# Seven products for the early chunks too, with weights ordered ahead of page reads

## Chip, cores, metric

The kernel runs on one core of a Trainium2 chip. The metric is the device time of one execution in microseconds (us). The program is written by hand for each engine: TensorE (PE in the profile), VectorE (DVE), ScalarE (ACT), GpSimd (POOL) and SyncE (SP, which here only issues transfers). Engines wait for each other through semaphores.

## What is computed

Two layers (DEPTH = 2) of a hybrid decoder trunk run over 512 prompt tokens and 8 x 8 sample tokens, 576 columns in all, in float32. Cut to what matters:

```python
h = rmsnorm(x, norm_g)
proj = h @ w_in                       # 1024 -> all branches at once
(lru_x, lru_z, nsa_q, nsa_kv, nsa_z, nsa_g,
 dn_qkv, dn_z, dn_a, dn_b, merge_g) = split(proj)
u = causal_conv(lru_x)                # 4 taps
out_lru = (rg_lru(u) * silu(lru_z)) @ w_lru_out
out_nsa = (sparse_attention(nsa_q, nsa_kv, pages, window) * silu(nsa_z)) @ w_nsa_out
qkv = silu(causal_conv(dn_qkv))       # 1536 channels, 4 taps
out_dn = (rmsnorm(gated_delta(l2norm(q), l2norm(k), v)) * silu(dn_z)) @ w_dn_out
merged = sum(sigmoid(merge_g_i) * out_i)
x = x + merged @ w_out
```

The sample rows also attend to a paged cache (8 pages of 128 rows for each of 8 samples) and to a window of 512 rows. Keys, values, states and convolution tails are outputs too.

## The kernel before

**The dense stream.** The projection is cut into chunks of 128 output channels. The list `UNITS` gives the order of all dense work of a layer: small gates and lx, then lz (4 chunks), dc (12), q (4), kv (6), nz (4), dz (4), then the merge gates mg with the output products ow between them, then wo. A unit fills one PSUM bank with 128 x 288 results, and units alternate between two banks (`u % 2`), so unit u waits until unit u - 2 is evicted by the engine named in the list ("A" for ACT, "V" for DVE). `dense()` yields after each matmul step (two records in the trace), and PE's program pulls steps from it with `fill(n, end)` and `dense_to(end)` between the small matmuls of the other stages. `take_to(end)` in ACT's and DVE's program evicts all units up to `end`; an engine takes them exactly where its program says so.

**Two ways to a pair of chunks.** For lx, lz and dc each chunk has two units (halves of the columns) of 8 steps: 32 steps to two chunks. For the kinds in `PAIRED` (q, kv, nz, dz, mg) two chunks are one 2 x 2 block product in seven products instead of eight (`PRODUCTS = "1627543"`), each of 4 steps: 28 steps. That needs sums of the activations (T2, T3, T4 in `tt`, and B12 - B11, written over B12), made once per layer, and sums of weights made by DVE for each pair: `weight_sums` (L1865) makes three in `ws` and in the ring slot, and runs right after product "5" of the pair before; `weight_sum` (L1874) makes the fourth after product "6". The results come out by additions of products in `sg` (L1783, L1786). DVE takes five of the seven products, ACT two.

**Weights.** `ring` holds two slots of two chunks each (1 MB), `owr` two output weights. SP's `weights(n)` (L593) waits until the pair in slot n - 2 is done (`slot_done`), `out_weights(n)` (L612) likewise for n - 2. SP works through its program in order, and the same program reads the cache: `cached_keys` (L650) and `cached_values` (L655) issue 16 transfers each with an address read from the page table, `window_keys` (L658) and `window_values` (L661) one per sample.

**Stages of a layer.** First the early stage: lx, lz and dc chunks with the convolutions (`conv`, L1847; `mix`, L1997, one per dc chunk) and the LRU recurrence on DVE, gates and SiLU on ACT. Then q, kv, nz, dz under the delta rule, then the rotary multiplies, then prompt attention (slots, L1292 to L1339), then the sample stage: four rounds of k2 with two samples each (L1371 to L1460). A round reads keys first, values later, and pulls 44 dense steps: the output products of one pair and the seven products of the next mg pair. `dext` is a ring of 7 chunk buffers that `mix` reads.

Of the kernel before, what the change touches and what calls it, by code (L numbers as in the profile page):

```python
# [138 lines left out]
EXTN = 7  # L139
# [64 lines left out]
def products(kind, c):  # L204
# [10 lines left out]
         + [(kind, c, h, who) for kind, n, who in (("lz", 4, "A"), ("dc", 12, "A")) for c in range(n) for h in range(2)]  # L215
         + [unit_ for kind, n in (("q", 4), ("kv", 6), ("nz", 4), ("dz", 4)) for c in range(0, n, 2) for unit_ in products(kind, c)]
# [20 lines left out]
PAIRED = ("q", "kv", "nz", "dz", "mg")  # L237
PAIRS = [(kind, c) for kind, c in SLOTS if kind in PAIRED]
NSUM = 4 + 4 * len(PAIRS)
# [30 lines left out]
def summed(l, k, which):  # L270

    return l * NSUM + {"first": 6, "S2": 7 + 4 * k, "S4": 8 + 4 * k}[which]

# [17 lines left out]
def chained(eng, done):  # L291
# [34 lines left out]
    s_pw=4, s_tr=8, s_tb=4, s_ta=4, s_mix=4, s_or=4, s_ot=4, s_z=8, dh_t=1, conv_ok=12, silu_ok=5, dc_ok=1, sp_abs=2,  # L326
    sp_exp=3, gb_ok=1, bm_ok=10, s0_in=128, p_z=5, p_y=5, p_g=20, p_e=5, p_x=5, p_s=5, p_d=5, p_k=15, p_b=5, i_w=31,
    i_wm=31, i_x=31, i_xm=31, f_mm=5, f_u=4, f_v=4, f_w=5, m_mm=3, u_mm=4, f_m=3, q_w=3, q_s=4, q_n=3, q_oe=4, b_gl=4,
    b_pe=7, b_so=1, b_vt=1, b_vn=1, b_vm=4, b_sn=4, dn_ok=1, mg_ok=32, small_in=96, sm_in=32, ln_ok=5, sum_ok=88,
# [3 lines left out]
def hybrid_trunk(nc, dram, out):  # L333

    ctx = ExitStack()
    with ctx:
# [178 lines left out]
        T2, T3, T4 = (tt[:, k] for k in range(3))  # L515
        S2, S3 = ws[:, 0], ws[:, 1]
# [5 lines left out]
        def factors(n, which):  # L522
# [32 lines left out]
        def chunk_half(kind, c, h):  # L555

            if kind == "kv":
                return hh(qk7[:, 4 + c // 2] if c % 2 == 0 else vT[:, c // 2], h)
            return hh(qk7[:, c] if kind == "q" else zs[:, {"nz": 4, "dz": 8}[kind] + c], h)
# [5 lines left out]
        def _(sp):  # L565
# [71 lines left out]
            for l in range(DEPTH):  # L637
# [43 lines left out]
                out_weights(l * NO + 3)  # L681
                sp.wait_ge(s["b_out"], l * 32 + 32)
# [162 lines left out]
        def _(pe):  # L845
# [11 lines left out]
            def dense():  # L857

                for u in range(DEPTH * N_ALL):
# [40 lines left out]
                    elif kind in PAIRED:  # L900
# [3 lines left out]
                        elif h == "6":  # L904
                            pe.wait_ge(s["sum_ok"], summed(l, k, "S2" if k else "first"))
                        elif h == "5" and k == 0:
                            pe.wait_ge(s["sum_ok"], summed(l, 0, "S2"))
                        elif h == "3":
                            pe.wait_ge(s["sum_ok"], summed(l, k, "S4"))
                        w, x = factors(g, h)  # L910
# [80 lines left out]
            for l in range(DEPTH):  # L991
# [24 lines left out]
                dense_to(u0 + U_DC + 4)  # L1016
# [3 lines left out]
                for n in range(8):  # L1020
# [9 lines left out]
                    fill(2, u0 + U_Q)  # L1030
# [447 lines left out]
        def _(act):  # L1478
# [32 lines left out]
            for l in range(DEPTH):  # L1511
# [3 lines left out]
                def take_to(end):  # L1515

                    for u in range(gone[0], end):
# [10 lines left out]
                        if kind == "lz":  # L1528
                            ins = A(hh(zs[:, c], h), ps, ACT.Silu)
                        elif kind == "dc":  # L1530
                            if h == 0 and c == 0 and u >= N_ALL:
                                act.wait_ge(s["xs_out"], 16 * (u // N_ALL))
                            if h == 0 and c >= EXTN:
                                act.wait_ge(s["conv_ok"], past["conv_ok"] + c - EXTN + 1)
                            e = dext[:, c % EXTN]
                            if h == 0:
# [861 lines left out]
```

## Time and profile before

| | |
|---|---|
| median of 3 runs | 2092.81 us (2089.54 to 2092.93) |
| the profiled execution | 2090.35 us, span on the core 2088.5 us |
| granted TensorE clock, mean | 0.945 |
| PE / DVE / ACT busy | 1842.8 / 946.0 / 515.9 us |
| HBM read / written | 153.67 / 21.71 MB |

In the profile a busy PE is one whose matmuls are in flight; "SPq" rows are transfers that SP issues, with the time the issuing takes. Bracketed figures in a timeline are the idle time before the row and what ended it.

### The profile page before, as it was taken

How to read it: one execution, taken by the hardware profiler on the slowest of the kernel's cores; microseconds unless marked ns; L12 is line 12 of the kernel's file. 1: busy time of each engine (PE TensorE's matmuls, PEld its weight loads, DVE VectorE, ACT ScalarE, POOL GpSimd, SP SyncE). 2: the span in 40 equal slices, each digit the busy share in tenths (PEclk: the TensorE clock that was granted, in tenths of full speed). 3: DMA queues.
4: the chain of work that ended last, by engine and by line, in shares of the span. 5: the costliest groups of instructions: out<-in, count | busy, mean ns of one | idle time of the engine just before them, and what ended most of it. 6: DMA issues, size and time to landing. Idle time of an engine off the chain costs nothing.

```text
span 2088.5 us, 29550 instructions
## 1 busy us (share of the span) xinstructions
PE 1842.8 (88%) x11486; PEld 1323.4 (63%) x11486; DVE 946.0 (45%) x2208; ACT 515.9 (25%) x1161; POOL 91.5 (4%) x133
## 2 busy tenths in 40 slices
PE   7999999998499955599999999999984998655999
PEld 5777787875355644477467767888652556444763
DVE  2558546336265432243135675453462653333421
ACT  3143211123266310110112341111322662110100
POOL 0001000011000000000000010100120000000000
PEclk9999999989799987899999999999997999887999
DMA  6214111123410233426042141111333103443321
GB/s 214 67 60 106 42 42 42 56 72 85 129 51 11 82 110 101 133 89 187 1 162 64 61 106 42 26 37 56 109 92 104 31 11 93 123 118 97 113 88 46
DMA packets 196528, 170.07 MB, mean 81 GB/s; under 512 B 49248, under 2 KB 186898, under 8 KB 195942
## 3 DMA queue, kind: packets, MB, share of 16 engines
q1 hardware_dynamic: 192164, 150.11, 24.7%
q0 software_dynamic: 4064, 18.03, 2.7%
q8 instruction: 91, 1.49, 0.3%
q14 instruction: 47, 0.39, 0.1%
q10 hardware_dynamic: 162, 0.05, 0.0%
HBM read 153.67 MB, written 21.71 MB: 84 GB/s over the span
## 4 chain that ended last, share of the span: by engine, by line
PE 75%; DVE 10%; SPq 7%; issue 4%; DMA 3%; ACT 1%; ACTq 0%; DVEq 0%
PE PS L920 49%; PE PS L849 5%; SPq L643 3%; DVE arena L1854 3%; DMA ring<-in_w_in 3%; SPq L655 3%; PE PS L1292 2%; PE PS L1305 2%; PE PS L1140 1%; PE PS L1122 1%; DVE arena L1780 1%; PE PS L1142 1%; PE PS L1361 1%; PE PS L1211 1%; PE PS L1026 1%
## 5 line engine op out<-in xcount | busy, mean ns | idle before, releaser
L920 PE MATMUL PS<-hT,ring 128*128 128x288 f32 x2624 | 692.3, 411 | 6.4 <-DVE arena L2057 3.7
L920 PEld LDWEIGHTS PS<-hT,ring 128*128 128x128 f32 x2624 | 488.4, 191 | 143.9 <-issue 11.7
L920 PE MATMUL PS<-zs,owr 128*128 128x288 f32 x768 | 215.6, 424 | 126.2 <-DVE sg L1786 126.2
L920 PEld LDWEIGHTS PS<-zs,owr 128*128 128x128 f32 x768 | 143.5, 197 | 170.5 <-DVE sg L1786 127.6
L920 PE MATMUL PS<-tt,ws 128*128 128x288 f32 x672 | 190.4, 415 | 11.8 <-DVE sg L1910 4.4
L849 PE MATMUL PS<-con,arena 128*128 128x128 f32 (+5 forms) x934 | 148.5, 286 | 13.4 <-DMA arena<-in_nsa_k_norm 10.7
L849 PEld LDWEIGHTS PS<-con,arena 128*128 128x128 f32 (+5 forms) x934 | 111.6, 144 | 74.2 <-issue 46.0
L920 PEld LDWEIGHTS PS<-tt,ws 128*128 128x128 f32 x672 | 120.7, 190 | 51.9 <-DVE sg L1910 8.0
L1786 DVE TENSOR_TENSOR ws<-ring 128x512 f32<-128x512 f32 x84 | 58.1, 691 | 201.8 <-DMA ring<-in_w_in 200.3
L920 PE MATMUL PS<-arena 128*128 128x512 f32 (+1 forms) x320 | 124.8, 594 | 2.1 <-DVE sg L1910 2.1
L1783 DVE TENSOR_TENSOR sg<-PS,sg 128x288 f32<-128x288 f32 x132 | 60.3, 457 | 134.6 <-PE PS L920 132.6
L920 PE MATMUL PS<-tt,ring 128*128 128x288 f32 x336 | 103.6, 443 | 11.3 <-DVE sg L1783 11.3
L1292 PE MATMUL PS<-arena 64*128 64x128 f32 (+3 forms) x256 | 53.1, 493 | 60.0 <-ACT arena L1713 60.0
L1854 DVE SCALAR_TENSOR_TENSOR arena<-arena,par 128x512 f32<-128x512 f32 x192 | 99.5, 518 | 6.8
L1713 ACT ACTIVATE arena<-PS,sm 128x128 f32<-128x128 f32 (+3 forms) x128 | 66.8, 524 | 128.6 <-DVE sm L2251 122.6
L920 PEld LDWEIGHTS PS<-arena 128*128 128x128 f32 (+1 forms) x320 | 52.9, 180 | 70.9 <-issue 67.9
L920 PEld LDWEIGHTS PS<-tt,ring 128*128 128x128 f32 x336 | 65.4, 205 | 32.4 <-DVE sg L1783 12.2
L2251 DVE CUSTOM_DVE_ANT_0 PS<-PS,con 128x128 f32<-128x128 f32 (+3 forms) x128 | 61.9, 505 | 44.2 <-PE PS L1292 44.2
L1292 PEld LDWEIGHTS PS<-arena 64*128 64x128 f32 x256 | 20.1, 193 | 85.9 <-ACT arena L1713 67.8
L1704 ACT ACTIVATE arena<-arena,sm 128x128 f32<-128x128 f32 (+3 forms) x128 | 64.7, 553 | 23.2 <-DVE sm L1780 23.2
L1786 DVE TENSOR_TENSOR arena<-arena,PS 128x512 f32<-128x512 f32 (+3 forms) x70 | 43.4, 622 | 59.0 <-PE PS L1142 36.7
L1780 DVE TENSOR_TENSOR arena<-arena 128x2304 f32<-128x2304 f32 (+3 forms) x24 | 39.7, 1656 | 58.1 <-ACT arena L1594 22.2
(303 smaller groups left out, 2060.9 us busy)
## 6 DMA issues: line engine op xcount, KB each, us to landing
ring<-in_w_in SPq DMA_DIRECT2D x54, 1024.0 KB, 5.4
arena<-in_cache_nsa_kv SPq DMA_DIRECT2D x128, 192.0 KB, 2.5
ring<-in_w_in SPq DMA_DIRECT2D x32, 256.0 KB, 4.3
arena<-in_state_nsa_win SPq DMA_DIRECT2D x32, 256.0 KB, 3.3
arena<-in_cache_nsa_kv SPq DMA_DIRECT2D x128, 64.0 KB, 1.8
arena<-in_w_out SPq DMA_DIRECT2D x4, 2048.0 KB, 8.1
out_win_sample<-in_state_nsa_win POOLq DMA_DIRECT2D x2, 4032.0 KB, 23.1
arena<-in_x_prompt SPq DMA_DIRECT2D x8, 512.0 KB, 5.3
```

Of the source, the lines that this page charges most:

```text
L643: at_page = sp.value_load(pgt[0:1, b * PAGES + k:b * PAGES + k + 1], min_val=0, max_val=N_PHYS - 1)
L655: sp.dma_start(page(b % 2, k)[:, 3 * P:4 * P], page_of(b, k)[:, 3 * P:4 * P]).then_inc(s["cv_in"], 16)
L849: return nc.tensor.transpose(dst, src, ident[0:src.shape[0], 0:src.shape[0]])
L920: ins = mm(to, w, x, start=start, stop=stop, skip_group_check=True)
L1292: mm(PS[:, 4 + g, 0:q0 + P], qk7[m, r, q0:q0 + P], qk7[m, 5 + br, 0:q0 + P], start=True, stop=True).then_inc(s["a_s"], 1)
L1704: A(p, p, ACT.Copy, scale=sm8[:, 7, u % 8:u % 8 + 1]).then_inc(s["a_n"], 1)
L1713: A(pring[slot % PRING][:, 0:width], PS[:, 4 + slot % 2, 0:width], ACT.Exp, scale=-1.0, bias=sm8[:, 0, k:k + 1], accum_out=sm8[:, 1, k:k + ...
L1780: return V.tensor_tensor(dst, a, b, ALU.mult)
L1783: return V.tensor_tensor(dst, a, b, ALU.add)
L1786: return V.tensor_tensor(dst, a, b, ALU.subtract)
L1854: ins = stt(out=d, in0=e, scalar=w(j), in1=d, op0=ALU.mult, op1=ALU.add)
L2251: V.tensor_tensor_reduce(out=raw, in0=raw, in1=C("causal")[:, 3 * P - q0:4 * P], scale=-1.0, scalar=-NEG, op0=ALU.add, op1=ALU.min, accum_ ...
```

## The change

The pairs of lz and dc join `PAIRED`, so that their 16 chunks are made by seven products each pair; "early" pairs (`k < N_EARLY`) take a separate T1 = B12 - B11, in `zs`, while lx units still read B12 whole; B12 itself is overwritten only at the first q pair. T1 to T4 are made before the lz chunks. DVE makes the early weight sums as it does for later pairs. ACT no longer evicts lz with SiLU but in a pass over `zs` later; products "5" and "3" of a dc pair are written to `dext` in two instructions. The steps of DVE's convolutions and LRU passes, and of ACT's activations, are cut into pieces with `take_to` between them. Mixes 10 and 11 move behind the first units of q. PE pulls three steps and not two after each LRU gate matmul. In the rotary multiplies DVE takes units in between.

In SP's program the weights move ahead: `weights(22)` before the wait for rotated keys, output weights and `weights(23)` between the first cached keys and values, and in each round of k2 `weights(25 + k2)` ahead of the wait for the keys, and the output weights between keys and values.

```diff
-         + [(kind, c, h, who) for kind, n, who in (("lz", 4, "A"), ("dc", 12, "A")) for c in range(n) for h in range(2)]
-         + [unit_ for kind, n in (("q", 4), ("kv", 6), ("nz", 4), ("dz", 4)) for c in range(0, n, 2) for unit_ in products(kind, c)]
+         + [unit_ for kind, n in (("lz", 4), ("dc", 12), ("q", 4), ("kv", 6), ("nz", 4), ("dz", 4)) for c in range(0, n, 2) for unit_ in products(kind, c)]
...
-PAIRED = ("q", "kv", "nz", "dz", "mg")
+PAIRED = ("lz", "dc", "q", "kv", "nz", "dz", "mg")
...
+        T1 = zs[:, 4:6, :].rearrange("p c (h t) -> p (c h) t", h=2)
...
-                    "4": (quarter(n, 1, 1), T4), "5": (quarter(n, 1, 0), B12), "6": (S2, T2), "7": (S3, T3)}[which]
+                    "4": (quarter(n, 1, 1), T4), "5": (quarter(n, 1, 0), T1 if early else B12), "6": (S2, T2), "7": (S3, T3)}[which]
...
+                weights(l * NS + 22)
                 sp.wait_ge(s["b_out"], l * 32 + 32)
                 sp.wait_ge(s["dn_ok"], past["dn_ok"] + 1)
                 sp.wait_ge(s["qk_ok"], past["qk_ok"] + 2)
                 cached_keys(0)
                 window_keys(0)
+                out_weights(l * NO + 4)
+                out_weights(l * NO + 5)
+                weights(l * NS + 23)
                 cached_values(0)
                 window_values(0)
-                for g in (22, 23, 24):
-                    weights(l * NS + g)
-                    for o in range(2):
-                        out_weights(l * NO + 2 * (g - 20) + o)
+                out_weights(l * NO + 6)
+                out_weights(l * NO + 7)
+                weights(l * NS + 24)
+                out_weights(l * NO + 8)
+                out_weights(l * NO + 9)
...
                 for k2 in range(DEC_BATCH // 2):
+                    weights(l * NS + 25 + k2)
                     if k2 < DEC_BATCH // 2 - 1:
                         sp.wait_ge(s["s_t"], past["s_t"] + 6 * (k2 + 1))
                         cached_keys(k2 + 1)
                         for b in (2 * k2 + 2, 2 * k2 + 3):
                             window_keys(b)
+                    for o in range(2):
+                        out_weights(l * NO + 10 + 2 * k2 + o)
+                    if k2 < DEC_BATCH // 2 - 1:
                         sp.wait_ge(s["s_pv"], past["s_pv"] + k2 + 1)
                         cached_values(k2 + 1)
                         for b in (2 * k2 + 2, 2 * k2 + 3):
                             window_values(b)
-                    weights(l * NS + 25 + k2)
-                    for o in range(2):
-                        out_weights(l * NO + 10 + 2 * k2 + o)
...
-                    fill(2, u0 + U_Q)
+                    fill(3, u0 + U_Q)
...
+                            elif kind == "dc" and h == "4":
+                                ins = sub(dext[:, (c + 1) % EXTN, HIST:HIST + HALF], sg[:, 2], ps)
+                            elif kind == "dc":
+                                e, summand = (dext[:, (c + 1) % EXTN], sg[:, 2]) if h == "5" else (dext[:, c % EXTN], sg[:, 1])
+                                cut = SEQ - HALF
+                                add(e[:, HIST + HALF:HIST + SEQ], ps[:, 0:cut], summand[:, 0:cut])
...
+                weight_sums(l, 0)
...
-                mix(0)
-                mix(1)
+                take_to(u0 + U_DC + 7)
+                mix(0, (8, 8, 9, 9))
+                mix(1, (10, 10, 11, 11))
+                take_before("lgp", 8)
                 dve.wait_ge(s["lg"], past["lg"] + 8)
-                link(mul(lb[:], lb[:], lu[:]))
+                for c in range(4):
+                    mul(lb[:, c], lb[:, c], lu[:, c])
+                    if c % 2:
+                        take_to(u0 + U_DC + 13 + c // 2)
+                mix(2, (15, 15, 16, 16))
+                mix(3, (17, 17, 18, 18))
...
+                mix(4, (22, 22, 23, 23))
+                mix(5, (24, 24, 25, 25))
...
-                link(V.tensor_tensor_scan(lh.rearrange("p c t -> p (c t)"), la.rearrange("p c t -> p (c t)"),
-                                          lb.rearrange("p c t -> p (c t)"), 0.0, ALU.mult, ALU.add))
...
+                for c in range(4):
+                    link(V.tensor_tensor_scan(lh[:, c], la[:, c], lb[:, c], 0.0, ALU.mult, ALU.add))
+                    ins = mul(zs[:, c], zs[:, c], lh[:, c])
+                    if c < 3:
+                        take_to(u0 + U_DC + 29 + c)
...
-                for c in range(3, 12):
-                    if c == 11:
-                        weight_sums(l, 0)
-                    mix(c)
+                mix(6, (32, 32, 33, 33))
+                mix(7, (34, 34, 35, 35))
+                mix(8, (36, 36, 37, 37))
+                mix(9, (38, 39, 40, 41))
+                take_to(u0 + U_Q)
                 dve.wait_ge(s["pj"], u0 + U_Q)
+                dve.wait_ge(s["sum_ok"], summed(l, N_EARLY, "S2"))
                 sub(B12, B12, B11).then_inc(s["sum_ok"], 1)
+                mix(10, (43, 43, 44, 44))
+                mix(11, (45, 45, 46, 46))
...
                 mul(zs[:, 8:12], zs[:, 8:12], dc[:, 0:4]).then_inc(s["dn_ok"], 1)
+                normed = began[("bc_ok", past["bc_ok"] + 10)]
+                take_to(normed + 1)
...
                     if n == 0:
                         take_before("kt_t", 2)
+                    else:
+                        take_to(normed + 2)
                     link(mul(x, x, rep(C("cos"), m - n)))
```

## Rows read from the trace of the kernel before

**Rows 1.** Waits of the whole trace: us in total, times, longest us.
```profile
DVE ws L1786 <- DMA ring<-in_w_in: 200.3, 10, 27.2
...
PE PS L920 <- DVE sg L1786: 126.2, 6, 21.8
```

**Rows 2.** Timeline of PE, sample stage of layer 0: start, length, instruction.
```profile
698.43 1.96 PE L1371 MATMUL PS<-arena,con 128*32 128x128 f32 x64 [0.84 <-issue]
...
735.18 1.95 PE L1371 MATMUL PS<-arena,con 128*32 128x128 f32 x64
...
758.49 2.29 PE L920 MATMUL PS<-zs,owr 128*128 128x288 f32 x4 [20.77 <-DVE sg L1786]
...
795.24 1.96 PE L1371 MATMUL PS<-arena,con 128*32 128x128 f32 x64
```

**Rows 3.** Timeline of DVE, attention and sample stages of layer 0.
```profile
561.95 0.69 DVE L1786 TENSOR_TENSOR ws<-ring 128x512 f32<-128x512 f32 x1 [26.98 <-DMA ring<-in_w_in]
...
731.29 0.46 DVE L1783 TENSOR_TENSOR sg<-PS,sg 128x288 f32<-128x288 f32 x1 [1.01 <-PE PS L920]
755.55 0.69 DVE L1786 TENSOR_TENSOR ws<-ring 128x512 f32<-128x512 f32 x1 [23.80 <-DMA ring<-in_w_in]
```

**Rows 4.** Timeline of SP's issues, the same stages.
```profile
520.05 17.25 SPq L650 DMA_DIRECT2D arena<-in_cache_nsa_kv  x16
...
556.24 0.51 SPq L610 DMA_DIRECT2D ring<-in_w_in  x1
...
707.70 17.15 SPq L650 DMA_DIRECT2D arena<-in_cache_nsa_kv  x16
724.89 0.99 SPq L658 DMA_DIRECT2D arena<-in_state_nsa_win  x2
729.86 17.22 SPq L655 DMA_DIRECT2D arena<-in_cache_nsa_kv  x16
...
748.16 0.51 SPq L610 DMA_DIRECT2D ring<-in_w_in  x1
748.71 1.58 SPq L626 DMA_DIRECT2D owr<-in_w_dn_out  x2
```

**Rows 5.** Timeline of PE, rotary multiplies and attention of layer 0.
```profile
503.43 4.04 PE L920 MATMUL PS<-tt,ring 128*128 128x288 f32 x8 [5.64 <-DVE sg L1783]
507.31 2.10 PE L920 MATMUL PS<-hT,ring 128*128 128x288 f32 x8
...
566.02 0.80 PE L1292 MATMUL PS<-arena 64*128 64x128 f32 x4 [28.96 <-ACT arena L1713]
```

**Rows 6.** Windows after two stops: length, busy PE, PEld, DVE, ACT, POOL, clock, DMA.
```profile
566.00:574.00 8.00, 7.98 (x32) 5.08 (x33) 3.35 (x17) 3.94 (x15) 0.00 (x0) 0.62 0.00 0
...
758.00:764.00 6.00, 5.51 (x17) 4.06 (x18) 2.08 (x4) 0.93 (x2) 0.00 (x0) 0.57 0.00 0
```

**Rows 7.** Window over most of the early stage of layer 0.
```profile
88.00:188.00 100.00, 100.00 (x414) 78.48 (x413) 67.00 (x151) 34.71 (x62) 0.00 (x0) 1.00 0.23 63
```

**Rows 8.** Timeline of PE, early stage of layer 0.
```profile
44.38 58.47 PE L920 MATMUL PS<-hT,ring 128*128 128x288 f32 x240
...
188.05 0.27 PE L849 MATMUL PS<-con,cst 128*27 128x128 f32 x1
```

**Rows 9.** Timeline of DVE, early stage of layer 0.
```profile
141.33 2.55 DVE L1780 TENSOR_TENSOR arena<-arena 128x2304 f32<-128x2304 f32 x1
...
144.60 4.96 DVE L2037 TENSOR_TENSOR_SCAN arena<-arena 128x2304 f32<-128x2304 f32 x1
...
156.62 0.17 DVE L1999 COPY arena<-arena 128x24 f32<-128x24 f32 x1
...
161.00 0.17 DVE L1999 COPY arena<-arena 128x24 f32<-128x24 f32 x1
...
187.27 0.69 DVE L1786 TENSOR_TENSOR ws<-ring 128x512 f32<-128x512 f32 x1
...
189.21 0.17 DVE L1999 COPY arena<-arena 128x24 f32<-128x24 f32 x1
```

More of the change, by code:

```diff
@@ L270, in summed, with product_unit @@
 def summed(l, k, which):
-    return l * NSUM + {"first": 6, "S2": 7 + 4 * k, "S4": 8 + 4 * k}[which]
+    return l * NSUM + (8 + 4 * N_EARLY if which == "T1" else
+                       {"S2": 7, "S4": 8}[which] + 4 * k + (k > N_EARLY or k == N_EARLY and which == "S4"))
+def product_unit(l, k, which):
+    return l * N_ALL + FIRST[PAIRS[k]] + PRODUCTS.index(which)
 def merged(n):
@@ L1015, in _ @@
                 ins.then_inc(s["gt_t"], 1)
-                dense_to(u0 + U_DC + 4)
+                dense_to(u0 + U_DC + AHEAD)
                 pe.wait_ge(s["con_in"], CON_IN * l + 16)
@@ L1527, in take_to @@
                         ps = PS[:, u % 2, 0:HALF]
[L1528 to L1536, printed above, removed]
-                                ins = A(e[:, HIST:HIST + HALF], ps, ACT.Copy)
-                            else:
-                                A(e[:, HIST + HALF:HIST + SEQ], ps[:, 0:SEQ - HALF], ACT.Copy)
-                                ins = A(e[:, HIST + SEQ:EXT].rearrange("p (b t) -> p b t", t=S_EXT)[:, :, HIST:],
-                                        ps[:, SEQ - HALF:HALF].rearrange("p (b t) -> p b t", t=DEC_SEQ), ACT.Copy)
-                        elif h == "1":
+                        if h == "1":
                             act.wait_ge(s["pv"], taken(u - 1, "V"))
@@ L1547, in take_to @@
                             ins = A(sg[:, 0], ps, ACT.Tanh, scale=0.5)
+                        elif kind == "dc":
+                            if c == 0 and u >= N_ALL:
+                                act.wait_ge(s["xs_out"], 16 * (u // N_ALL))
+                            if c >= EXTN:
+                                act.wait_ge(s["conv_ok"], past["conv_ok"] + c - EXTN + 1)
+                            ins = A(dext[:, c % EXTN, HIST:HIST + HALF], ps, ACT.Copy)
                         else:
@@ L1862, in conv @@
                                 link(ins)
+                        take_to(units[j])
                 def weight_sums(l_, k):
@@ L1983, in _ @@
                 V.memset(dext[:, :, 0:HIST], 0.0)
+                dve.wait_ge(s["sum_ok"], past["sum_ok"] + 2)
+                sub(T4, T2, B21).then_inc(s["sum_ok"], 1)
+                sub(T1, B12, B11).then_inc(s["sum_ok"], 1)
                 take_to(u0 + U_LZ)
                 dve.wait_ge(s["pv"], taken(u0 + U_LZ, "V"))
+                weight_sums(l, 0)
                 for c in range(4):
-                    conv(lu[:, c], lext[:, c], lambda j: prm("lconv", 4 * j + c), prm("lcb", c), s["u_ok"])
+                    conv(lu[:, c], lext[:, c], lambda j: prm("lconv", 4 * j + c), prm("lcb", c), s["u_ok"],
+                         [u0 + U_LZ + min(4 * c + j, U_DC - U_LZ) for j in range(CONV_W)])
                 def tails(dst, ext):
@@ L1995, in _, with mix @@
                     tails(cst[:, c], lext[:, c])
-                def mix(c):
+                def mix(c, units):
                     e = dext[:, c % EXTN]
@@ L2005, in mix @@
                         ins.then_inc(s["dc_ok"], 1)
-                    conv(dc[:, c], e, lambda j: prm("dconv", 12 * j + c), None, s["conv_ok"])
+                    conv(dc[:, c], e, lambda j: prm("dconv", 12 * j + c), None, s["conv_ok"], [u0 + U_DC + at for at in units])
                 x = spb[:, 5, :].rearrange("p (k h) -> p k h", h=DN_H)
@@ L2012, in _ @@
                 stt(out=spb[:, 0, :], in0=spb[:, 5, :], scalar=-1.0, in1=spb[:, 5, :], op0=ALU.mult, op1=ALU.max).then_inc(s["sp_abs"], 1)
-                for n, (dst, a, b, op) in enumerate(((T3, B22, B12, sub), (T2, T3, B11, add), (T4, T2, B21, sub))):
-                    if n:
-                        dve.wait_ge(s["sum_ok"], past["sum_ok"] + n)
-                    op(dst, a, b).then_inc(s["sum_ok"], 1)
+                take_to(u0 + U_DC + 2)
                 dve.wait_ge(s["sp_exp"], past["sp_exp"] + 3)
@@ L2192, in _ @@
                         take_before("kt_t", 3)
+                    else:
+                        take_to(normed + 3)
                     add(x, x, y).then_inc(s["qk_ok"], 1)
```

95 lines of the change are left out of this document (62 added, 33 removed).

## Prediction

> **What bounds the kernel now.** The waits come first. TensorE (PE) is the busiest engine, and six times it stands still before the products `PS<-zs,owr`, 126.2 us in all, behind a weight sum of VectorE (DVE); DVE itself stands ten times, 200.3 us in all, for `ring<-in_w_in` to land [rows 1]. No other wait of PE is of that size, so I read the timeline at those places.
>
> The sample stage runs in four rounds of k2. Its first matmuls (L1371) start at 698.43, 735.18 and 795.24: the first round takes 36.75 us, the second 60.06, for the same work [rows 2]. In the second PE stops for 20.77 us before 758.49 [rows 2]. DVE took a product at 731.29, and then waited 23.80 us for the ring, until 755.55 [rows 3]: `take_to` runs `weight_sums` of the next pair right after product 5, and in order. SyncE (SP) shows why the ring is late: it issues 16 cached keys at 707.70 (17.15 us), window keys at 724.89, 16 cached values at 729.86 (17.22 us), and only at 748.16 the weights, at 748.71 the two output weights [rows 4]. The slot of those weights had been free since the round began; they stand behind 32 page reads. So PE waits for DVE, DVE for a transfer, and the transfer for its place in SP's program.
>
> The same happens once in the attention stage: weights are issued at 556.24 behind keys that began at 520.05 [rows 4], DVE waits 26.98 us for them [rows 3], PE 28.96 us [rows 5]. A smaller stop of another kind, 5.64 us before 503.43, ends with a product taken by DVE [rows 5], which was in the rotary multiplies.
>
> Each stop costs more than its length. After the two long ones the granted clock was 0.62 in 566 to 574 and 0.57 in 758 to 764, with PE busy nearly throughout [rows 6]: PE started at 1.2 GHz and came back to 2.4 some 5 to 7 us later.
>
> The early stage, where the new products go, is different. PE is busy 100.00 of 100 us there at full clock, DVE 67.00 [rows 7]. It goes from 56.1 (44.38 and three units of 3.9 us) to 188.05 [rows 8], 131.9 us.
>
> **The change, part by part, for one layer.** Layer 1 repeats layer 0, so everything counts twice.
>
> *Fewer matmuls.* 240 records take 58.47 us, 0.2436 each, two records to a matmul step [rows 8]. A pair of chunks now takes 4 units of 8 steps, and will take 7 units of 4: 28 instead of 32. Eight pairs (lz 2, dc 6) drop 32 steps, 32 x 0.487 = 15.6 us. PE alone would need 131.9 - 15.6 = 116.3 us, 13.6 to a pair.
>
> *More for DVE in those same microseconds.* A pair costs five evictions at 0.46 [rows 3], a fourth sum at 0.69, and three sums of which 187.27 to 189.21 shows the length, 1.94 [rows 9]: 4.9 us, and about 0.3 for two evictions that are split in two in dc. ScalarE (ACT) loses its evictions, which it had time for anyway. A `mix` takes 161.00 - 156.62 = 4.38 us [rows 9]; a pass over four LRU chunks 2.55, the scan 4.96 [rows 9]. From the third dc pair on, DVE owes, between the units that it must take:
> - pair 3: mixes 2 and 3 (8.8), the pair (5.2), two LRU passes (5.1): 19.1
> - pair 4: mixes 4 and 5 (8.8), 5.2, one pass (2.6): 16.5
> - pair 5: mixes 6 and 7 (8.8), 5.2, small steps (0.9), scan (5.0), one pass (2.6): 22.4
> - pair 6: mixes 8 and 9 (8.8), 5.2: 14.0
>
> That is 72.0 us against 4 x 13.6 = 54.6 of PE. There are two PSUM banks, so PE can lead by two units at most, and it waits for the other 17.4 us. In the four pairs before, DVE's load (two convolutions or two mixes and the products, 13 to 15 us a pair) lies inside PE's time, stretched in the second dc pair by the LRU gates; only the very first weight sums hold PE up, about 0.7. So the early stage takes 116.3 + 17.4 + 0.7 = 134.4 us, 2.5 more than before: the saved matmuls are spent on waiting for DVE. Mixes 10 and 11 then fall behind the stage, together with the moved B12 difference, so that `conv_ok` 12, the last SiLU and the squares come some 5 us later relative to the q pair; PE has other units to fill there, and I take 1.5. Sum: +4. Bounds: -12 if DVE's steps overlap so well that PE sets the pace after all (then only the first sums and the q pair cost), +12 if each of the 24 handovers of these pairs costs DVE some 0.3 us more than rows of undisturbed runs show.
>
> *Weights ahead of page reads.* In a round without a stop PE needs 36.75 us. SP's load per round is 17.2 + 1.0 + 17.2 + 1.0 + 0.5 + 1.6 = 38.5 us [rows 4]. I walk it from S, the start of the first round. `weights(25)` goes before S, since its slot is free. Keys S+9.3 to S+26.5 (as 707.70 is to 698.43), window keys to 27.5, output weights to 29.1, values from S+31.4 (729.86) to 48.6, window values 49.6, then `weights(26)` 50.1, keys to 67.3, window keys 68.3, output weights 69.9, values to 87.1, and once more the same to 106.8 for the last keys and 108.4 for output weights. PE starts rounds at S+36.75, 73.5 and 110.25. It wants keys at the start, which were issued by 27.5, 68.3 and 106.8; ring weights (through DVE) 33 us into a round, issued 20 us before that; values some 26 us into a round, with more than 10 us to spare; output weights about 2 us into a round, issued by 29.1, 69.9, 108.4 and hence 3 to 4 us ahead of need in the last round, about what a landing takes. So the three stops go, and SP, slower than PE by 1.8 us a round, just keeps ahead for the three rounds. Saved: second round 60.06 - 36.75 = 23.3, which holds the stop and the 2.5 of low clock behind it, three times: 70; I give back 1 for the last output weights: 69. Bounds 56 (5 us left in each round) and 71.
>
> *Weights 22 before the wait for keys.* Slot 20 is free after the matmuls at 507.31 (2.10 us), ahead of the keys at 520.05 [rows 4, 5], so the weights land before DVE asks. The stop of 28.96 goes, and the 3.4 lost at a clock of 0.5 after it: 32.4. What is late next is the output weights of that pair, now behind 16 keys and not 32 transfers: issued at 538 to 539, wanted at about 542. I take 31, bounds 26 and 32.4.
>
> *Takes between the rotary multiplies.* The product that ended the 5.64 us stop is taken right after the gating product; a later one waits about 2 us behind a multiply, and rotated rows come some 3 us later. I take 4 of the 5.64 plus low clock, bounds 0 and 7.
>
> Per layer: +4 - 69 - 31 - 4 = -100; two layers -200. The profiled execution took 2090.35 (span 2088.5), which gives 1890; the median of the runs shown is 2.5 above it, so 1892.
>
> **A rule that speaks against it.** The early stage would have many short stops of PE where it has none now. The rows show full clock where PE never stops [rows 7] and the lower one behind stops of 20 us and more [rows 6]; stops of 1 to 3 us, as forecast here, have no row of their own. The Trainium skill (TensorE: Matmul & The Clock Gate, section "A second HAM failure mode: psum-queue depth-cycling") says that cycling through PSUM banks with small idles between groups of matmuls can make the clock oscillate between its two levels. By that rule this stage would fall to the lower clock again and again, which is the third rival below; I take full clock, since each unit between two stops is 1.95 us of dense matmuls.
>
> **Rivals.**
> 1. The early stage keeps its 15.6 us (DVE overlaps after all): -12 instead of +4 per layer, 1892 - 32 = 1860. For it: DVE has 33 idle us in 100 there [rows 7]. Against: the added work is uneven, and three of the last four pairs hold more than a pair's time.
> 2. SP becomes the bound in the sample stage. It has 38.5 us of issues for 36.75 of PE; the weights share queues with page reads. If each of the six later rounds keeps 5 us, and the attention stop another 4, the time is 1892 + 30 + 8 = 1930.
> 3. The lower clock holds in dc pairs 3 to 6. A pair then takes PE 27.3 us instead of DVE's 18.0, so 9.3 x 4 x 2 = 74: 1966, if it holds throughout; 1930 at half of that.
> 4. Slower than before. SP's order puts `out_weights` between keys and values, and `weights(23)`, which waits for slot 21, ahead of the first values. Should such a wait close a ring (values late, so PE late, so the slot late), each round would be paced by it. It decides only beyond the 23.3 us that a round saves: values would have to land 34 us later than in the walk. Paced at 65 us a round it gives 1892 + 6 x 28 = 2060, and with the attention stop kept 2120. Nothing in the walk comes near it.
> 5. The reordering does nothing, because the transfer and not its issue is late: 1892 + 200 = 2092 or so. Against: 7 us pass from issue to DVE's start (748.16 to 755.55) [rows 3, 4], and 17 in SP's issues.
>
> **How the numbers follow.** Chances: the forecast 0.55, rival 1 0.15, rival 2 0.18, rival 3 0.08, rivals 4 and 5 0.04 together. The reordering's gain is common to the first four cases. The forecast's own bounds, not all at once, reach from 1870 to 1920; the range takes in rival 1 and most of rival 2 and leaves the lower clock out: 1858 to 1932. Faster by over 0.2% (about what a measurement of this kernel can tell from no change) 0.96, within it 0.015, slower 0.025.
>
> **What would show it.** L1371 starts about 37 us apart in all rounds, DVE's waits for `ring<-in_w_in` nearly gone from 200 us, granted clock 1.00 from 510 us on through the stage; these carry 180 of the 200 us. In the early stage PE busy near 85%, with waits for DVE (sums, stt lines of the convolution) from the third dc pair on, and the q pair starting 2 to 3 us later than 188 us. If PE is busy throughout there, rival 1 holds. If the granted clock falls below 1.00 there, rival 3. If PE stops before `owr` products for a DMA and not for DVE, rival 2. The prediction is wrong if the sample rounds differ from each other by more than 5 us.

## The result and the profile after

| | before | after |
|---|---|---|
| median | 2092.87 us (4 runs) | 1903.22 us (1899.25 to 1905.93, 4 runs) |
| profiled execution, span | 2090.35, 2088.5 us | 1899.25, 1897.5 us |
| granted clock, mean | 0.945 | 0.989 |
| PE / DVE busy | 1842.8 / 946.0 us | 1805.1 / 1021.6 us |

The ratio is 0.9093, 95% interval 0.9073 to 0.9114: 190 us less. The forecast was 1892, range 1858 to 1932.

The waits of the whole trace come first, as in [rows 1]: us in total, times, longest us. The first three rows are PE's largest, then come the one of the rotary multiplies and the row of DVE that had 200.3 us.

```profile
PE PS L933 <- DVE arena L1802: 11.7, 6, 2.5
PE PS L933 <- DVE arena L2115: 11.0, 2, 5.5
PE PS L933 <- DVE sg L1799: 10.8, 11, 2.3
...
PE PS L933 <- DVE sg L1802: 4.2, 2, 2.1
...
DVE ws L1802 <- DMA ring<-in_w_in: 1.8, 2, 1.2
```

The weights have gone from 200.3 us of DVE's waiting to 1.8, and PE's 126.2 us behind weight sums are gone with them. New are waits of another kind, for evictions (L1799, L1802) and for a copy at L2115. Now PE's timeline, layer 0, at the places of [rows 2], [rows 5] and [rows 8].

```profile
43.83 13.85 PE L933 MATMUL PS<-hT,ring 128*128 128x288 f32 x56
...
130.06 2.21 PE L933 MATMUL PS<-tt,ring 128*128 128x288 f32 x8 [0.57 <-DVE sg L1799]
132.10 2.10 PE L933 MATMUL PS<-hT,ring 128*128 128x288 f32 x8
136.68 3.90 PE L933 MATMUL PS<-hT,ring 128*128 128x288 f32 x8 [2.48 <-DVE arena L1802]
140.41 2.10 PE L933 MATMUL PS<-tt,ws 128*128 128x288 f32 x8
...
168.05 2.21 PE L933 MATMUL PS<-tt,ring 128*128 128x288 f32 x8 [2.28 <-DVE sg L1799]
...
175.15 2.21 PE L933 MATMUL PS<-hT,ring 128*128 128x288 f32 x8 [2.24 <-DVE arena L1802]
...
190.76 0.27 PE L862 MATMUL PS<-con,cst 128*27 128x128 f32 x1
...
206.40 4.21 PE L933 MATMUL PS<-hT,ring 128*128 128x288 f32 x8 [5.49 <-DVE arena L2115]
...
509.78 1.24 PE L933 MATMUL PS<-zs,owr 128*128 128x288 f32 x4 [2.08 <-DVE sg L1802]
...
540.43 0.49 PE L1305 MATMUL PS<-arena 64*128 64x128 f32 x4 [1.89 <-ACT arena L1729]
...
670.16 1.96 PE L1384 MATMUL PS<-arena,con 128*32 128x128 f32 x64 [0.84 <-issue]
...
706.90 1.96 PE L1384 MATMUL PS<-arena,con 128*32 128x128 f32 x64
...
743.65 1.96 PE L1384 MATMUL PS<-arena,con 128*32 128x128 f32 x64
...
780.46 1.96 PE L1384 MATMUL PS<-arena,con 128*32 128x128 f32 x64
...
783.52 1.21 PE L933 MATMUL PS<-zs,owr 128*128 128x288 f32 x4 [0.52 <-DMA owr<-in_w_dn_out]
```

The rounds start 36.74, 36.75 and 36.81 us apart: the three long stops are gone, and so is that of 28.96 us in the attention, of which 1.89 us are left. The early stage, which had no stop, now has them, the longest 2.48 us.

SP's issues in the last round it feeds, to set against [rows 4]: keys, window keys, output weights, values, window values, ring weights.

```profile
760.90 17.05 SPq L657 DMA_DIRECT2D arena<-in_cache_nsa_kv  x16
778.00 0.98 SPq L665 DMA_DIRECT2D arena<-in_state_nsa_win  x2
779.02 1.05 SPq L633 DMA_DIRECT2D owr<-in_w_dn_out  x2
780.86 17.22 SPq L662 DMA_DIRECT2D arena<-in_cache_nsa_kv  x16
798.12 1.15 SPq L668 DMA_DIRECT2D arena<-in_state_nsa_win  x2
799.31 0.51 SPq L617 DMA_DIRECT2D ring<-in_w_in  x1
```

PE took these output weights at 783.52 after a wait of 0.52 us (above): SP is just in time, with nothing over.

Last the windows (columns as in [rows 6]): the quiet and the crowded part of the early stage, to set against [rows 7], then three short ones.

```profile
88.00:121.00 33.00, 33.00 (x137) 25.72 (x136) 23.08 (x65) 11.52 (x19) 0.00 (x0) 1.00 0.14 43
121.00:190.70 69.70, 57.59 (x219) 41.43 (x219) 66.77 (x153) 19.85 (x32) 0.00 (x0) 0.98 0.23 60
...
137.00:141.00 4.00, 4.00 (x11) 2.83 (x10) 3.85 (x11) 0.34 (x1) 0.00 (x0) 0.58 0.47 162
166.00:178.00 12.00, 6.83 (x25) 4.53 (x26) 11.44 (x33) 0.61 (x2) 0.00 (x0) 1.00 0.39 75
206.50:213.00 6.50, 6.50 (x27) 3.55 (x28) 2.33 (x4) 4.71 (x8) 6.38 (x12) 0.58 1.02 285
```

From 121 us on DVE is busy 66.77 of 69.70 us and PE 57.59: DVE sets the pace there. In these windows the clock is 1.00 but for one fall behind the stop of 2.48 us, and a second in the q pair. From 510 to 890 us, attention and sample stage, it was 1.00 throughout, as forecast.

**Where the time went, layer 0.** Each row is the difference of the same two landmarks in both traces.

| stretch | before | after | change | forecast |
|---|---|---|---|---|
| early stage, to the conv tails' matmul | 131.9 | 135.2 | +3.3 | +2.5 |
| q pair, to the first delta-rule matmul (223.0; 230.2) | 34.9 | 39.4 | +4.5 | +1.5 |
| to the output products behind the rotary multiplies (509.25; 509.78) | 286.3 | 279.6 | -6.7 | -4 |
| to the first round | 189.2 | 160.4 | -28.8 | -31 |
| rounds, to the first wo matmul (988.48; 890.89) | 290.1 | 220.7 | -69.3 | -69 |

The sum, with 0.6 us less ahead of the early stage, is -97.6 us; layer 1 gave -93.4 (its rounds -67.2). Of the -6.7 only 5.0 belong to the rotary multiplies (from 495.69 to 509.25 before, from 501.25 to 509.78 after). The other 1.6 lie in the delta rule, 272.7 us before and 271.1 after: both kernels have a stretch at half clock there (last section), and in layer 0 of the kernel before it was some 3 us longer.

### The profile page after: what moved, and what is told of

It reads as the page before. It is cut to its first block, busy times and chain, and to the rows that moved or that the text cites. A ratio compares the mean times of both kernels' runs of the same rounds, so it can differ in the third digit from the quotient of the medians.

```text
span 1897.5 us, 29614 instructions
## 1 busy us (share of the span) xinstructions
PE 1805.1 (95%) x11358; PEld 1283.6 (68%) x11358; DVE 1021.6 (54%) x2414; ACT 505.7 (27%) x1133; POOL 91.3 (5%) x133
## 4 chain that ended last, share of the span: by engine, by line
PE 77%; DVE 14%; SPq 4%; issue 3%; ACT 1%; DMA 0%; ACTq 0%; DVEq 0%
PE PS L933 50%; PE PS L862 5%; DVE arena L1871 3%; PE PS L1305 2%; PE PS L1318 2%; SPq L650 2%; DVE arena L1796 2%; PE PS L1153 1%; PE PS L1135 1%; DVE ws L1802 1%; PE PS L1155 1%; SPq L657 1%; PE PS L1224 1%; PE PS L1374 1%; PE PS L1246 1%
## 5 line engine op out<-in xcount | busy, mean ns | idle before, releaser
L933 PE MATMUL PS<-hT,ring 128*128 128x288 f32 x1984 | 549.3, 416 | 27.0 <-DVE arena L1802 11.7
L933 PEld LDWEIGHTS PS<-hT,ring 128*128 128x128 f32 x1984 | 366.8, 192 | 138.7 <-DVE arena L1802 14.4
L933 PE MATMUL PS<-tt,ws 128*128 128x288 f32 x928 | 259.1, 413 | 14.3 <-DVE sg L1928 4.4
L933 PEld LDWEIGHTS PS<-tt,ws 128*128 128x128 f32 x928 | 168.6, 190 | 70.5 <-issue 9.4
L1799 DVE TENSOR_TENSOR sg<-PS,sg 128x288 f32<-128x288 f32 x164 | 74.9, 457 | 147.7 <-PE PS L933 145.7
L933 PE MATMUL PS<-tt,ring 128*128 128x288 f32 x464 | 133.5, 423 | 7.5 <-DVE sg L1799 7.4
L1543 ACT ACTIVATE sg<-PS 128x288 f32<-128x288 f32 x58 | 23.4, 403 | 337.9 <-PE PS L933 337.7
L933 PEld LDWEIGHTS PS<-tt,ring 128*128 128x128 f32 x464 | 86.4, 195 | 36.2 <-DVE sg L1799 11.7
L933 PEld LDWEIGHTS PS<-arena 128*128 128x128 f32 (+1 forms) x320 | 52.7, 179 | 71.1 <-issue 68.1
L1802 DVE TENSOR_TENSOR ws<-ring 128x512 f32<-128x512 f32 x116 | 80.1, 691 | 3.9 <-DMA ring<-in_w_in 1.8
L1802 DVE TENSOR_TENSOR arena<-arena,PS 128x512 f32<-128x512 f32 (+3 forms) x70 | 43.3, 621 | 58.1 <-PE PS L1155 36.7
L1535 ACT ACTIVATE sg<-sg 128x288 f32<-128x288 f32 x72 | 31.2, 436 | 120.2 <-DVE sg L1799 105.1
```

The source lines that it names most:

```text
L933: ins = mm(to, w, x, start=start, stop=stop, skip_group_check=True)
L1799: return V.tensor_tensor(dst, a, b, ALU.add)
L1802: return V.tensor_tensor(dst, a, b, ALU.subtract)
```

## Experiments

**The order alone, and the rest alone.** Does the reordering carry the gain, and what do the products add?

```diff
 # order_only: the kernel before, with SP's program of the changed kernel
+                weights(l * NS + 22)
...
+                    weights(l * NS + 25 + k2)
...
 # products_only: the changed kernel, with SP's program of the kernel before
-                weights(l * NS + 22)
...
-                    weights(l * NS + 25 + k2)
...
```

> The kernel before with the new order of SyncE's transfers alone (weights 22 ahead of the keys, weights and output weights ahead of page reads in the rounds); no new products, no new takes. Theory (the order carries the whole gain): the sample stage of a layer loses 69 us and the attention stop 29 us, so 2093 - 2 x 98 = 1897 us, and DVE's waits for the ring go from 200 us to under 10. Rival (the order needs the other edits to pay, because the rotary takes or the products bring the keys forward): the stops go only in part, above 1930 us.

Measured: 1894.55 us, ratio 0.9055 (0.9032 to 0.9078). All long stops are gone, DVE waits 2.8 us in all for the ring, and the rotary stop is still there: PE's timeline of this kernel.

```profile
501.17 3.25 PE L926 MATMUL PS<-tt,ring 128*128 128x288 f32 x6 [5.64 <-DVE sg L1789]
```

> The changed kernel with the transfers in the old order. Theory (the early stage is bound by DVE, so the seven products cost about 8 us a layer up to the second q pair and the rotary takes give 6 to 7 back): 2090 to 2100 us, with the rounds of the sample stage 36.7, 60, 61 us again. Rival (the 15.6 us a layer of dropped matmuls are really saved and something later hides it): near 2062 us.

Measured: 2102.75 us, the median of six runs (2101.63 without one of 2141.53), ratio 1.005 (1.0027 to 1.0073), a little above what was expected. PE's timeline shows the early stop, the one of the q pair and one of the rounds.

```profile
137.06 1.24 PE L927 MATMUL PS<-hT,ring 128*128 128x288 f32 x4 [2.48 <-DVE arena L1796]
...
206.80 1.81 PE L927 MATMUL PS<-hT,ring 128*128 128x288 f32 x3 [5.50 <-DVE arena L2109]
...
761.64 2.29 PE L927 MATMUL PS<-zs,owr 128*128 128x288 f32 x4 [21.14 <-DVE sg L1796]
```

The two ratios multiply to 0.910, which is the changed kernel's: the parts hardly meet. The order brings the whole gain; all the rest together (products, rotary takes and the steps cut to make room for them) loses time.

**The takes in the rotary multiplies alone**, on top of the order.

```diff
 # order_only, and:
+                normed = began[("bc_ok", past["bc_ok"] + 10)]
+                take_to(normed + 1)
...
                         take_before("kt_t", 2)
+                    else:
+                        take_to(normed + 2)
...
```

> The kernel before with the new order of transfers and the takes between the rotary multiplies, lz and dc as before (32 steps for two chunks). Theory: the early stage returns to 131.9 us and the q pair to 22.3, so 1903 - 2 x 7.8 = 1888 us, faster than the changed kernel. Rival (the seven products pay after all): at or above 1903, up to 1903 + 31 = 1934 us.

Measured: 1885.62 us, ratio 0.9004 (0.8981 to 0.9028), 9 us below order_only on the same chip. The rotary stop is 2.08 us, as in the changed kernel. This version keeps eight plain units for a pair of early chunks, and is the fastest here together with lz_pairs (below): 12.2 us less in span than the changed kernel (1885.3 against 1897.5), 17.6 in the medians. The stretch of the q pair is 34.9 us again; the 22.3 of the expectation is not this stretch.

**The weight sums of the early pairs.** If DVE's sums are what costs the 15.6 us of saved matmuls, nearly free sums must bring them back. In this kernel each early sum is made over 4 of the 128 columns of a block, so the results of the early pairs are not those of the reference; PE, evictions and transfers are as in the changed kernel; `ws` is set to zero once, ahead of all.

```diff
+            V.memset(ws[:], 0.0)
...
+                    m = 4 if k < N_EARLY else P
...
-                    sub(S3, quarter(n, 0, 0), quarter(n, 1, 0)).then_inc(s["sum_ok"], 1)
+                    sub(S3[:, :, 0:m], quarter(n, 0, 0)[:, :, 0:m], quarter(n, 1, 0)[:, :, 0:m]).then_inc(s["sum_ok"], 1)
...
```

> The changed kernel, with the weight sums of the lz and dc pairs made of 4 columns in each of 4 blocks and not 128, so that the sums of the early pairs are left out in the main: 0.17 us and not 0.69 each, with the same waits and the same order. Theory (VectorE's load sets the early stage's pace): of the 17 us over PE's time some 2 us a pair go, the early stage falls from 135.2 to about 127 us, the total to about 1887 us. Rival (PE waits for the handovers between engines and for the places of the takes, not for the load): early stage within 2 us of 135, total 1900 to 1903 us.

Measured: 1885.39 us, ratio 0.9008 (0.8986 to 0.903). The early stage takes 56.9 to 183.53 us, 126.6. A window over its crowded part:

```profile
121.00:183.00 62.00, 54.45 (x215) 39.80 (x214) 59.11 (x150) 19.97 (x32) 0.00 (x0) 1.00 0.25 67
```

8.6 us come back, not 19 (135.2 down to the 116.3 of PE alone): DVE is busy 59.11 of 62.00 us even so. Evictions, mixes and LRU passes fill it. The stage is now 5.3 us shorter than with plain units (131.9), but in the q pair PE stops for 5.39 us here too, and that stretch takes 38.0 and 38.5 us in the two layers instead of 34.9. So in all, seven products with nearly free sums only tie with the plain units of order_rope.

**The order cut in two.** Its two places, each without the other, on the kernel before.

```diff
 # rounds_order: the loop over k2 only
+                    weights(l * NS + 25 + k2)
...
 # first_order: all that stands ahead of that loop only
+                weights(l * NS + 22)
...
```

> The kernel before with the new order in the four rounds of the sample stage only; the attention stage's transfers as before. Theory: the three long rounds of a layer fall to 36.8 us, 69 us a layer, 2094 - 138 = 1956 us, and the stop of 29 us in attention stays. Rival (the late weights of attention carry over, so that the rounds start behind): over 1970 us.

Measured: 1952.59 us, ratio 0.9336 (0.9311 to 0.9361).

> The kernel before with the new order up to the attention stage only (weights 22 ahead of the keys, output weights and weights 23 between keys and values); the rounds as before. Theory: the attention stop of 29 us and the low clock behind it go, two times 29 to 31: 2094 - 60 = 2034 us; rounds of 36.8, 60, 61, 60 us stay. Rival: the stop moves to the output weights or to a wait for the first values and the gain is under 10 us a layer, over 2074 us.

Measured: 2029.51 us, ratio 0.9709 (0.9688 to 0.973). The rounds of layer 0 stay as they were (36.8, 59.5 and 61.3 us). The two timelines, first rounds_order, then first_order, each with what its half leaves or mends:

```profile
562.99 0.80 PE L1293 MATMUL PS<-arena 64*128 64x128 f32 x4 [28.99 <-ACT arena L1714]
```

```profile
538.91 0.49 PE L1297 MATMUL PS<-arena 64*128 64x128 f32 x4 [1.89 <-ACT arena L1718]
```

The halves bring 138 and 61 us (from 2090.5), together the 199 of order_only; the forecast had 2 x 69 and 2 x 31.

**Only the ring's weights ahead in a round**, the output weights left behind the values.

```diff
 # order_only, but in the loop over k2:
-                    for o in range(2):
-                        out_weights(l * NO + 10 + 2 * k2 + o)
                     if k2 < DEC_BATCH // 2 - 1:
...
+                    for o in range(2):
+                        out_weights(l * NO + 10 + 2 * k2 + o)
```

> The kernel before with the new order, but in the rounds only the ring weights go ahead; the output weights are issued behind the cached values, as before. Theory of the walk: output weights are wanted 2 us into the next round and issued some 10 us after that, so PE stops about 16 us in each of three rounds for the transfer itself and not for DVE; of 69 us a layer about 21 are left, and 29 in attention: 1993 us. Rival (only the ring weights, through DVE's sums, hold the rounds up): 1895 us.

Measured: 1994.13 us, ratio 0.9533 (0.9514 to 0.9551). Its waits:

```profile
PE PS L926 <- DMA owr<-in_w_dn_out: 89.3, 6, 15.8
```

The stops are back in all six rounds, for the next transfer in the same queue. Of the rounds' 138 us, 100 hang on the place of the output weights (1994.1 against 1894.6). Moving only the weights that the trace named wins 38 of the 138.

**The stop of 5.49 us in the q pair.** It ends with the copy at L2115, behind mixes 10 and 11 on DVE. First, 12 steps of dense work ahead of PE's wait, where 4 stood behind it.

```diff
 # q_fill
+                fill(12, u0 + U_MG0)
                 pe.wait_ge(s["lo_ok"], past["lo_ok"] + 3)
-                fill(4, u0 + U_MG0)
```

> The changed kernel, in which PE pulls 12 dense steps before it waits for VectorE's copy of the convolution rows and for the squares, where it pulled none there and 4 behind that wait. Theory (the stop of 5.49 us in the first q pair is only that wait, since mixes 10 and 11 stand behind the stage): the stop and the low clock behind it go, 4 to 6 us a layer, 1903 - 10 = 1893 us. Rival (the chain mix 11, SiLU, squares is late by itself and the stop moves on to the norms): 1900 to 1903 us.

Measured: 1940.02 us, ratio 0.9275 (0.9258 to 0.9293). Neither theory had this: 37 us lost. The stop did shrink to 1.97 us, but new ones stand far behind it. PE's timeline:

```profile
474.12 2.29 PE L933 MATMUL PS<-zs,owr 128*128 128x288 f32 x4 [5.79 <-DVE arena L1799]
...
498.15 2.29 PE L933 MATMUL PS<-hT,ring 128*128 128x288 f32 x4 [4.36 <-ACT sg L1543]
...
557.77 2.74 PE L933 MATMUL PS<-zs,owr 128*128 128x288 f32 x5 [5.82 <-DMA owr<-in_w_lru_out]
```

The stream now runs 8 steps ahead of the places where the other programs take and issue. To test that, the next kernel pulls as many in all as the changed one.

```diff
 # q_shift
+                fill(12, u0 + U_MG0)
                 pe.wait_ge(s["lo_ok"], past["lo_ok"] + 3)
-                fill(4, u0 + U_MG0)
                 square_sums(past, "dn", "sum", dsq[:, 0:4])
-                fill(4, u0 + U_MG0)
                 square_sums(past, "dn_k", "sum", dsq[:, 4:8])
-                fill(6, u0 + U_MG0)
+                fill(2, u0 + U_MG0)
```

> The changed kernel, in which PE pulls 12 dense steps ahead of its wait for the copied rows of the q pair, and 8 fewer behind it, so that the stream stands where it did from the broadcasts on. Theory A (the 37 us that 12 steps ahead without the later ones taken away cost came from the stream running 8 steps ahead of DVE and the transfers downstream): the stop of 5.49 us becomes one of about 2 us, the half clock behind it goes, nothing is lost later, 4 to 5 us a layer, 1894 us. Theory B (the loss came from pulling the steps in this place): 1925 us or more. That it is hidden behind the squares of ACT, which end at 209.4: 1900 to 1903.

Measured: 1895.21 us, ratio 0.9057 (0.9028 to 0.9086). The loss is gone, so it was the stream's lead and not the place. The first delta-rule matmul starts at 225.81 us, 34.9 after the early stage as in the kernel before, and the clock stays full:

```profile
206.92 2.21 PE L933 MATMUL PS<-hT,ring 128*128 128x288 f32 x8 [1.96 <-DVE arena L1798]
```

Whether it is faster than the changed kernel stays open: the intervals overlap, and the spans differ by 2.1 us only. Two things eat into the 4.5 and 3.3 us that the q pairs of the two layers win. In layer 0 the clock falls behind the stops of 2.08 and 1.89 us of the rotary multiplies and the attention (0.62 in 505.5 to 510, 0.66 in 536 to 541), where it stayed full in the changed kernel; and PE, being earlier, waits more for SP in the last rounds (1.26 us for output weights, 2.74 for cached keys).

Second, mixes 10 and 11 without taps 1 and 2, and without tap 3 on the prompt columns, so that their channels are not the reference's.

```diff
 # short_mixes, in conv
+                            if short and j and (j < CONV_W - 1 or k == 0):
+                                continue
...
```

> The changed kernel, in which mixes 10 and 11 leave out taps 1 and 2, and tap 3 of the prompt columns, so that DVE has some 5.8 us less between the early stage and the copy of the rows; their rows of the result are not those of the reference. Theory (the stop of 5.49 us and the half clock behind it come from these two mixes, which stand ahead of the copy on DVE): the copy comes at 201 to 203, the stop shrinks to about 2 us, the stretch to the first delta-rule matmul from 39.4 to about 34.5 us, 1893 us. Rival (the copy's own work and the second matmuls of the rows set the time, not the mixes): stop of 5 us stays, 1900 to 1903.

Measured: 1896.13 us, ratio 0.9066 (0.9044 to 0.9088). The stretch shrank from 39.4 to 35.2 us (192.70 to 227.90), the stop to 2.34 us, but the clock still fell behind it:

```profile
177.10 2.89 PE L933 MATMUL PS<-hT,ring 128*128 128x288 f32 x8 [2.24 <-DVE arena L1802]
179.79 3.21 PE L933 MATMUL PS<-tt,ws 128*128 128x288 f32 x8
...
205.20 3.67 PE L933 MATMUL PS<-hT,ring 128*128 128x288 f32 x8 [2.34 <-DVE arena L2117]
```

So the mixes hold the copy up. What the 4.2 us are worth in the end is not settled: from there to the first round this execution took 443.3 us, against 440.0 in the changed kernel, and its span is 1898.5 us, with a start 2.0 us later. The 3.3 went into the clock. Both executions have the same stops in the rotary multiplies (2.08 us, then 0.63) and in the attention (1.89). Behind them the clock stayed full in the changed kernel and fell in this one, for about 1.7 us of lost time each. The windows, first two of the changed kernel, then two of short_mixes:

```profile
511.50:516.00 4.50, 4.35 (x25) 3.67 (x26) 4.46 (x5) 1.98 (x4) 1.13 (x2) 1.00 0.37 127
540.00:545.00 5.00, 4.57 (x29) 3.14 (x30) 2.58 (x14) 3.81 (x16) 0.00 (x0) 1.00 0.63 188
...
509.20:514.00 4.80, 4.64 (x17) 3.72 (x18) 4.17 (x5) 1.14 (x2) 1.13 (x2) 0.64 0.33 114
539.80:545.00 5.20, 5.17 (x22) 3.12 (x23) 2.03 (x12) 2.48 (x9) 0.00 (x0) 0.67 0.42 120
```

**Seven products for lz alone**, where DVE has room, on top of order_rope; ACT's SiLU of lz moves as in the change.

```diff
 # order_rope, and:
+         + [unit_ for c in range(0, 4, 2) for unit_ in products("lz", c)]
+         + [("dc", c, h, "A") for c in range(12) for h in range(2)]
...
+PAIRED = ("lz", "q", "kv", "nz", "dz", "mg")
```

> The kernel with the new order and the takes between the rotary multiplies, and seven products for the two lz pairs only, where VectorE's load lies inside TensorE's time; dc as before, mixes in their old places. Theory (the products pay exactly where VectorE has room): 8 steps of 0.487 us a layer are saved, less about 0.7 for the first sums: 1885.6 - 6.5 = 1879 us. Rival (pairs in the early stage cost as much as they save wherever they stand): 1885 to 1890 us.

> The kernel with the new order and the takes between the rotary multiplies once more, beside lz_pairs on the same chip: 1883 to 1888 us.

Measured: lz_pairs 1885.96 us, ratio 0.9018 (0.9005 to 0.903); order_rope again, beside it, 1887.93 us, 0.9032 (0.902 to 0.9044). The 2 us between them are within the intervals, so neither the theory nor its rival is shown by the times. In the trace the early stage is 1.7 us shorter in either layer, of the 3.2 expected. The first round starts 5.4 us earlier (659.5 against 664.9), but 3.3 of that is the stretch at half clock in the delta rule, which happened to be shorter (clock 0.87 in 418 to 444, against 0.74 in 420 to 446). The wo stage starts only 3.5 earlier (882.19 against 885.71), since in the last round PE waits for SP's transfers:

```profile
771.40 1.96 PE L1381 MATMUL PS<-arena,con 128*32 128x128 f32 x64 [1.60 <-DMA arena<-in_cache_nsa_kv]
...
774.82 1.21 PE L930 MATMUL PS<-zs,owr 128*128 128x288 f32 x4 [0.87 <-DMA owr<-in_w_dn_out]
```

## Why the prediction was right, step by step

The mechanism held and the sum was 9 us low against its own execution (1899.25 for 1890), 11 in the medians. The two terms that carry it, rounds and weights 22, came within 3 us a layer. The small ones came out less well, and two of their misses partly cancel: the q pair cost 3.0 us more than forecast, the rotary stretch gave up to 2.7 more.

- **Rounds, -69.** Measured -69.3 and -67.2. The walk of SP's queue held to 2 us: from S = 670.16 it put the values' end at 718.8 (measured 718.78) and the last window keys at 777.0 (778.98). The output weights of the last round were forecast 3 to 4 us ahead of need; PE waited 0.52 us for them. ring_only confirms the queue as the cause: the walk gave stops of about 16 us for it, and they are 15.8 at most. rounds_order shows that the term stands by itself.
- **Weights 22, -31.** Measured -28.8, first_order 61 us for two layers. The output weights that were named as late next did not hold PE up; 1.89 us of the stop stayed, behind ACT. I had counted the stop as gone.
- **Rotary takes, -4.** Measured -6.7 in that row of the changed kernel, of which 5.0 in the multiplies themselves, and 4.5 a layer between order_only and order_rope. The other 1.6 are luck: a stretch at half clock in the delta rule was longer in the kernel before. The forecast named the later take that waits: it is the stop of 2.08 us.
- **Early stage, +2.5.** Measured +3.3. The load of 72.0 us of DVE for four dc pairs was the right reading: PE takes 71.1 us over these four (119.62 to 190.76), DVE is 96% busy from 121 us on, and small_sums shows it 95% busy even with the sums nearly free. PE stands still for 12.1 us of the 17.4 that it was to wait; 1.8 more are the one fall of the clock, and the rest are units that run a little slower behind each stop. By the forecast's own list all four pairs hold more than a pair's time (the last 14.0 us against 13.6), not three. PE is busy 83% there; I had named 85% for the whole stage, where it is 91% from 60 us on.
- **q pair, +1.5: this term was mis-sized.** It measured +4.5 (layer 1: +4.4). I costed the mixes that fall behind the stage by the work that PE has in between, but did not name the wait that they stand ahead of. PE asks for the copied rows (`lo_ok`) before it pulls more dense steps, so the lateness of DVE's copy went into a stop of 5.49 us and a unit at half clock behind it. short_mixes and q_shift, which take away the one and the other, both bring the stretch back to 35 us.
- **Layer 1 "repeats layer 0".** It gave 4.2 us less: 2.1 in the rounds, where PE waited 1.43 us once for cached keys, and 1.6 in the delta rule, where layer 1 of the kernel before did not have the longer stretch at half clock.
- **"These carry 180 of the 200 us."** By the forecast's own terms the order carries 2 x (69 + 31) = 200, and order_only measured 199.

**Rivals.** The first, DVE overlaps after all, is excluded by PE's idle time from 121 us on. The second, SP as the bound, did not come, but its edge is reached: waits of 0.3 to 1.6 us for SP's transfers stand in the last rounds of this kernel, order_only and lz_pairs. The third, the lower clock, came for some 3 us once in the early stage of either layer and not throughout. The rule of the Trainium skill (TensorE: Matmul & The Clock Gate, section "A second HAM failure mode: psum-queue depth-cycling") warned of a clock that oscillates under such stops; over ten of them (0.44 to 2.48 us) the granted clock was 0.98, so here it costs little. The fourth and fifth found nothing: the same transfers, issued earlier, took the waits away.

**What the products cost.** Against order_rope the changed kernel's early stage is 3.3 us longer in either layer and its q pair 4.4: 15.5 us in all. The spans differ by 12.2 only, since in this execution of order_rope the clock fell twice in layer 0 where it stayed full in the changed kernel (last section), which cost it 3.1. By the medians it is 18. So the change is a gain of 199 us by order, 9 by the takes, and a loss of 12 to 18 by the products with the edits that make room for them. What dc's products would cost without those edits no run shows.

## What to carry to other kernels

- When a transfer is late, look where it stands in its queue's program before looking at its bandwidth: here one slot had been free for a whole round, behind 32 issues of 1.07 us. Walk the queue for all that it feeds: moving only the transfer that the trace names put the stop on the next one.
- Fewer matmuls are a gain only where the engine that feeds them has room in those same microseconds. An average (DVE 67% busy) hid four pairs with more than a pair's time of work. And even where DVE had room (lz alone) the gain stayed within what the runs can tell.
- Work moved behind a stage must be placed against the next wait of the busy engine; and filling a wait with steps from a shared stream shifts everything that other engines' programs place by that stream, which cost 37 us here.

## What was not expected of the hardware

The granted clock fell behind stops of 2 to 2.5 us, but not behind each. In the changed kernel it was 0.58 after the stop of 2.48 us (137 to 141 us; a unit of 8 records took 3.90 us, not 2.10), and stayed 1.00 from 166 to 178, with stops of 2.28 and 2.24 us and PE busy 6.83 of 12. In short_mixes the same stage ran 2 us later: behind the stop of 2.48 us the unit took 2.21, and the clock fell behind the one of 2.24, where two units took 2.89 and 3.21. In the q pair it fell behind stops of 5.49 and 2.34 us and not behind 1.96. It is not the program either. order_rope ran twice, with the same stops of 2.08, 0.63 and 1.89 us in layer 0: in the first execution the clock fell behind them (0.62, and 0.66 in 535 to 540), in the second it stayed full. One window of each, behind the stops of 2.08 and 0.63:

```profile
504.50:509.00 4.50, 4.29 (x15) 3.46 (x16) 3.72 (x5) 1.14 (x2) 1.14 (x2) 0.62 0.25 84
...
506.20:511.00 4.80, 4.65 (x26) 3.92 (x27) 4.77 (x5) 2.28 (x4) 1.17 (x3) 1.00 0.44 150
```

So two executions of one kernel can differ by 3 us in one stretch without a stop more or less, and a difference of that size between two spans says little. No run tells what decides it.

The clock also fell once in each layer of both kernels where PE did not stop at all, in the delta rule, while it ran 64 matmuls of 128x128 by 128x16. The kernel before, PE busy 10.00 of 10 us:

```profile
432.00:442.00 10.00, 10.00 (x38) 8.59 (x38) 0.88 (x2) 0.00 (x0) 4.41 (x3) 0.50 0.00 0
```

That stretch cost 3.4 us in lz_pairs, 5.1 in the changed kernel and 6.8 in the kernel before (layer 0; what it costs is half of its length). In order_rope's two executions it cost 5.2 and 6.8.
